# Two transformer stacks on one core: the eight squared chunks of each norm are summed on VectorE, then over partitions by one matmul

## What is computed

```python
def rmsnorm(x, g):
    xf = x.astype(jnp.float32)
    y = xf * lax.rsqrt(jnp.mean(xf * xf, axis=-1, keepdims=True) + NORM_EPS)
    return (y * g.astype(jnp.float32)).astype(x.dtype)

def swiglu(h, w_gu, w_down):
    gate, up = jnp.split(h @ w_gu, 2, axis=-1)
    return (jax.nn.silu(gate) * up) @ w_down
```

## Time and profile before

| | |
|---|---|
| device time, 3 runs | 3997.68, 3991.67, 3996.16 us; median 3996.16 us |
| span of the profiled execution | 3996.0 us; the profile gives no other time of this execution, and the span ends 0.16 us below the median run |
| mean granted TensorE clock | 0.954 of full speed |
| line 534 (norm sums) | 352 matmul records, two for each of 176 matmuls |
| HBM read | 648.56 MB, 163 GB/s over the span |

### The profile page before, as it was taken

The page is one execution under the profiler, slowest core; times in us unless marked ns, Lnnn a source line. Parts: engine busy times, 40 slices in busy tenths (PEclk is TensorE's granted clock), DMA queues, the critical chain, the costliest instruction groups (busy, mean ns, idle before and its releaser), DMA issues. The chain is left out here.

```text
span 3996.0 us, 67990 instructions
## 1 busy us (share of the span) xinstructions
PE 3679.5 (92%) x28562; PEld 3552.6 (89%) x28562; DVE 2434.3 (61%) x2565; ACT 1783.3 (45%) x2047; POOL 559.9 (14%) x208
## 2 busy tenths in 40 slices
PE   7998788999899998699999789899999889999999
PEld 7997688999899997599999689899999669999999
DVE  4575459797577776677777545554546544545644
ACT  3353255665355554355555234344443344444343
POOL 0001126462032330133310110000001000000000
PEclk9998798999999999899999899999999899999999
DMA  5542045565366663275744015445444215454453
GB/s 206 180 153 79 1 169 210 215 228 200 109 241 235 230 238 115 94 265 211 262 179 169 1 43 190 158 170 178 170 177 166 83 44 194 154 193 158 158 179 126
DMA packets 89670, 652.27 MB, mean 163 GB/s; under 512 B 10000, under 2 KB 10000, under 8 KB 10640
## 3 DMA queue, kind: packets, MB, share of 16 engines
q1 hardware_dynamic: 78480, 572.05, 39.3%
q0 software_dynamic: 11008, 77.60, 5.4%
HBM read 648.56 MB, written 1.05 MB: 163 GB/s over the span
## 5 line engine op out<-in xcount | busy, mean ns | idle before, releaser
L1348 DVE TENSOR_TENSOR w_lo<-raw,w_hi 128x2048 fp32r<-128x2048 f32 x540 | 1390.0, 2580 | 890.0 <-ACT w_hi L909 889.9
L498 PE MATMUL wrk<-h_hi,w_hi 128*128 128x256 f32 x5748 | 1649.5, 287 | 112.7 <-DVE h_lo L1360 68.2
L499 PE MATMUL wrk<-h_hi,w_lo 128*128 128x256 f32 x5748 | 1642.1, 286 | 0.0
L500 PE MATMUL wrk<-h_lo,w_hi 128*128 128x256 f32 x5748 | 1641.2, 286 | 0.0
L909 ACT ACTIVATE w_hi<-raw 128x2048 fp32r<-128x2048 f32 x540 | 1029.9, 1911 | 1047.1 <-PE wrk L500 975.1
L498 PEld LDWEIGHTS wrk<-h_hi,w_hi 128*128 128x128 f32 x5748 | 1120.0, 195 | 125.0 <-issue 118.9
L499 PEld LDWEIGHTS wrk<-h_hi,w_lo 128*128 128x128 f32 x5748 | 1120.3, 195 | 0.4 <-issue 0.2
L500 PEld LDWEIGHTS wrk<-h_lo,w_hi 128*128 128x128 f32 x5748 | 1119.4, 195 | 0.0
L498 PE MATMUL acc<-hid_hi,w_hi 128*128 128x256 f32 x2288 | 652.1, 285 | 21.3 <-DVE w_lo L1348 21.1
L499 PE MATMUL acc<-hid_hi,w_lo 128*128 128x256 f32 x2288 | 650.2, 284 | 0.0
L500 PE MATMUL acc<-hid_lo,w_hi 128*128 128x256 f32 x2288 | 650.1, 284 | 0.0
(11 more groups left out here) (244 smaller groups left out, 3065.5 us busy)
## 6 DMA issues: line engine op xcount, KB each, us to landing
raw<-in_wts SPq DMA_DIRECT2D x540, 1024.0 KB, 4.8
arena<-in_mods POOLq DMA_DIRECT2D x72, 1024.0 KB, 5.1
const<-in_const SPq DMA_DIRECT2D x1, 2176.0 KB, 10.0
c<-in_bias POOLq DMA_DIRECT2D x8, 256.0 KB, 2.9
x<-in_x SPq DMA_DIRECT2D x1, 1024.0 KB, 5.3
c<-in_c SPq DMA_DIRECT2D x1, 1024.0 KB, 5.1
out<-x SPq DMA_DIRECT2D x1, 1024.0 KB, 3.9
vec<-in_vec SPq DMA_DIRECT2D x1, 402.5 KB, 3.2
```

Source lines behind the costliest of these rows:

```text
L498: nc.tensor.matmul(o, wh, rh, start=first, stop=False, skip_group_check=True)
L499: nc.tensor.matmul(o, wl, rh, start=False, stop=False, skip_group_check=True)
L500: return nc.tensor.matmul(o, wh, rl, start=False, stop=last, skip_group_check=True)
L1348: tt(w_lo[:, ns % SLOTS, :], raw[:, ns % SLOTS, :], w_hi[:, ns % SLOTS, :].bitcast(F32), ALU.subtract).then_inc(lo_ready, 1)
```

## The change

TensorE's `norm_sum` becomes one matmul over `sq_sum`, and a new VectorE function `sum_squares` makes `sq_sum` (128 x 256) with one `tensor_reduce` over all 8 squared chunks. It waits for all four squares (and for the preceding norm's `rstd`). It reads the squares as "p t k": the 8 values that make one sum lie 1 KB apart in a partition.

```diff
--- before.py
+++ after.py
@@ -285,6 +285,7 @@
         const = sb("const", [P, NCONST])
         der = sb("der", [P, 2, 2, 9 * KC])
         rstd = sb("rstd", [P, NB])
+        sq_sum = sb("sq_sum", [P, T])
         arena = sb("arena", [P, ARENA])
         wrk = ctx.enter_context(nc.psum_tensor("wrk", [P, BANKS, NB], F32))
         acc = ctx.enter_context(nc.psum_tensor("acc", [P, BANKS, NB], F32))
@@ -363,6 +364,7 @@
         c_loaded = sem("c_loaded")
         sq_ready = sem("sq_ready")
         rstd_ready = sem("rstd_ready")
+        sq_summed = sem("sq_summed")
         h_ready = sem("h_ready")
         h_hi_ready = sem("h_hi_ready")
         h_lo_ready = sem("h_lo_ready")
@@ -524,15 +526,11 @@
                                      slab(s, q * 256, 256), q == 0 and t == 0, q == kc - 1)
                 return m.then_inc(w_used, 1)
 
-            def norm_sum(i, name, label="norm", nth=0, sq=sq):
+            def norm_sum(i, name, label="norm", nth=0):
 
                 o = bank(use[name, label])
-                sq0 = 4 * (before(i, "norm") + nth)
-                for k in range(KC):
-                    if k % 2 == 0:
-                        pe.wait_ge(sq_ready, sq0 + k // 2 + 1)
-                    m = nc.tensor.matmul(o[:, 0:T], cst("ones"), sq[:, k, :], start=(k == 0), stop=(k == KC - 1))
-                m.then_inc(filled, 1)
+                pe.wait_ge(sq_summed, before(i, "norm") + nth + 1)
+                nc.tensor.matmul(o[:, 0:T], cst("ones"), sq_sum[:], start=True, stop=True).then_inc(filled, 1)
 
             def down(ns, step, at=static, k=0, kh=0, first=False, last=False):
 
@@ -556,7 +554,7 @@
                 h0 = before(i, "h")
                 if "a" in prm:
                     across(ns, bank(u0), h_at=h0)
-                    norm_sum(i, name, sq=sq_late)
+                    norm_sum(i, name)
                 else:
                     norm_sum(i, name)
                     across(ns, bank(u0), h_at=h0)
@@ -1359,8 +1357,20 @@
                 dve.wait_ge(h_hi_ready, h0 + k + 1)
                 tt(h_lo[:, k, :], h[:, k, :], h_hi[:, k, :].bitcast(F32), ALU.subtract).then_inc(h_lo_ready, 1)
 
+            def sum_squares(i, nth=0, src=None):
+
+                n = before(i, "norm") + nth
+                dve.wait_ge(sq_ready, 4 * n + 4)
+                if n:
+                    dve.wait_ge(rstd_ready, n)
+                v = sq if src is None else src
+                nc.vector.tensor_reduce(sq_sum[:], v[:].rearrange("p k t -> p t k") if v is sq else v.rearrange("p k t -> p t k"),
+                                        AX.X, ALU.add).then_inc(sq_summed, 1)
+
             def normed(i, prm, nth=0, src=None, low=True):
 
+                if nth == 0:
+                    sum_squares(i)
                 xs = (src or stream(i))[0]
                 h0 = before(i, "h") + 8 * nth
                 if xs is c:
@@ -1395,6 +1405,8 @@
                             ts(h[:, k, :], xs[:, k, :], scale_cols(prm, k)[0], None, ALU.mult).then_inc(h_ready, 1)
                         if k:
                             h_low(h0, k - 1)
+                    split_to(ns + 1)
+                    sum_squares(i, src=sq_late)
                     split_to(ns + 2)
                     dve.wait_ge(rstd_ready, before(i, "norm") + 1)
                 else:
@@ -1859,6 +1872,8 @@
                     split_to(ns + q + 3)
 
                 for q, label in enumerate(CTX_PROJ):
+                    if q == 3:
+                        sum_squares(i, 1)
                     if q == 5:
                         normed(i, prm, nth=1, low=False)
                     place(q, label)
```

## The result

| | before | after |
|---|---|---|
| median of 4 runs each, same session | 3996.6 us | 4072.57 us (4069.73 to 4074.73) |
| ratio, 95% interval | | 1.0196 (1.0181 to 1.021) |
| span of the profiled execution | 3996.0 us | 4072.9 us |
| granted TensorE clock, mean | 0.954 | 0.938 |

The account below looks back on a forecast made before the run. VectorE's split chain was taken to bound plain openings, TensorE gate-first ones. Terms 35.9 + 8.8 + 3.6 - 2.0 + 1.8 = 48.1 us on 3996.0 gave 4044 us; own range 4028 to 4064, whole range 4028 to 4093.

Parts of the forecast that it names:

- What bounds it: At plain openings the path is update, square, w_hi, w_lo, h; the 3.61 us of norm sums lie beside it.
- plain openings: Norms where TensorE only runs the 8 sums, then idles; eight like mix_0 were to lose 4.49 us each, 35.9 us.
- The reduction, 2.29 us: VectorE's sum over 2048 values of a partition at each of 22 norms: 2.29 us, bounds 2.14 and 2.75 us.
- the rival: Strided read at half rate: 2.14 us more at 21 of the 22 reductions, +45 us, so 4089 us; 16 in 100.
- The turn: From the reduction's start until VectorE can go on: reduction 2.29, hand-over 0.10, slow matmul 1.20, Ln and Exp 0.90, 4.49 us.
- Waits that are swallowed first: Where VectorE already waits for rstd, less is added: b0_ctx 2.4 us, b0_ffn0 and the context norm 3.2 us each.
- the ends: The two ends, where no split lies in between: the change adds 1.8 us at each, 3.6 us together.
- Gate-first openings: Eight norms where TensorE's queue is full of gate products, norm sums and up products: gains and losses sum to +1.8 us.
- TensorE's time decides: Rival: reducing in VectorE's gap ahead of w_lo, plain openings cost nothing, gate-first ones gain 3.0 us each; 3974 us; 4 in 100.
- Level: Rival: rstd comes sooner than counted or later slack takes up the delays, within 8 us of before; 5 in 100.

## Why the prediction was right, and where not

**What bounds it.** Right. The matmuls lie beside other work at plain openings: putting them back costs nothing (4072.44 us). The path there is `w_hi`, `w_lo`, `h`, and all that the change puts on VectorE behind `w_lo` lengthens it.

**The reduction, 2.29 us.** This is the step that failed. I took it from the two-input subtraction and held 2.75 us for the upper bound; it is 3.65 us. The error, 1.36 us, comes 21 times: 28.6 of the 28.8 us between 48.1 and the measured 76.9. For neighbours 2.29 was right (2.28). So the price per value in my row was right, and what I left out was that its values lie side by side. The Trainium skill's note on cachelines ("SBUF — State Buffer", "Door 1: The DMA port swizzle") pointed there, and the trace agrees with its direction: 1.6 times as long at 512 B and at 1 KB. Of the 2.14 us that the rival added (half rate, 4.4 us) it is 64%. My forecast and this rival were two points, and the measured 4072.6 lies between them, outside the forecast's own 4028 to 4064. That it lies inside the whole range is owed to the range having been drawn past the rival's 4089, and not to the forecast.

**The turn.** Hand-over, low clock, Ln and Exp: 2.20 us forecast, 2.24 measured at the eight plain openings. The slow matmul (1.19 us) came as the idle time before it let one expect.

**Waits that are swallowed first.** Right within 0.2 us in all of b0_ctx, b0_ffn0, the context norm and the ends, once the reduction has its length.

**Gate-first openings.** Right in the sum (11.1 against 1.8 + 7 x 1.36 = 11.3, and 11.3 in a run of its own), right singly in five of eight. In three the split met GpSimd's products otherwise than before. That the place of the reduction gives the gain back was right in part: moved ahead of the split, this half of the change costs 3 us in place of 11, but the 3.0 us that I had expected to win at each opening did not come, since the split then waits.

**Rivals.** "TensorE's time decides" was priced at 3974 for a reduction in VectorE's hole; what I had for it is half right. In the hole the plain openings do cost little (0.5 us each with neighbours, 1.9 without), but the gate-first ones don't gain 3.0 each (3996.25 us for this half alone). That even a free reduction would only bring the change level in its present place was not tried; 28.6 us for 1.36 us each extrapolate to 4072.6 - 21 x 3.65 = 3995.9 (an estimate), which fits it. "Level" fell: `h` waits 2.24 us behind the reduction at mix_0, and the openings' costs stay.

## What to carry to other kernels

Work that an engine does while it would wait costs nothing, so taking it away gains nothing, while the same work put on the engine that is waited for costs its full length at each place. Price an operation by its access pattern too: find a row with the same distance between values, or put the strided case into the range as a factor. And before moving work, look for the hole of the receiving engine: the same reduction cost some 33 us less when it stood one split earlier at the plain openings.

## What the hardware showed that I had not expected

- VectorE's reduction of 2048 float32 values in a partition takes 2.28 us over neighbours and 3.65 us at 1 KB between values (3.59 at 512 B), with the same time for 128 or 256 sums.
- ScalarE pays for distance when it writes: squares of 512 values 616 ns in rows, 1159 ns when values go 32 bytes apart.
- A two-input operation on VectorE that starts just behind a GpSimd product is held up for about as long as that product takes (4.6 us), whatever its own size: two `h_lo` of 0.4 us took 9.47 us. One that started 0.04 us ahead was not touched (2.28 us), but those that started 0.44 us ahead and 0.17 us behind GpSimd's issue of a load took 7.2 us. The one-input reduction was never more than 0.2 us above its 3.65 (3.85 at most, beside a product).
- Eight matmuls ahead of 5.8 us of idleness left the next one at the low clock at mix_0 (1.22 us).
